# A two-layer hybrid encoder in hi/lo fp32r products: the feed-forward projections as 2x2 block products with seven multiplications

## The chip, the cores and the metric

The kernel runs on one core of one Trainium2 chip. The metric is the device time of one execution in microseconds (us), the median of several. PE is the matrix engine (PEld its weight loads), ACT the scalar engine, DVE the vector engine, POOL the general-purpose engine, SP the queue that issues DMAs. Each takes its instructions in order and waits at semaphores.

## The reference

The input x has 512 tokens of 1024 features. Layer 1 mixes by a gated delta rule over eight heads and by attention into 256 memory tokens; layer 2 by sliding-window attention over shared keys and values and by the same kind of memory attention. Each layer ends with a SwiGLU feed-forward network, and that is what is changed:

```python
def swiglu(h, w_gate_up, w_down):
    gate, up = jnp.split(h @ w_gate_up, 2, axis=-1)
    return (jax.nn.silu(gate) * up) @ w_down
```

Here h = rms_norm(x) is 512 x 1024, w_gate_up is 1024 x 5632, w_down is 2816 x 1024, and the result is added to x. Everything is float32.

## The kernel before

Activations lie transposed, features on the 128 partitions and the 512 tokens along the free axis, so that 1024 features are 8 tiles of 128 x 512 and the 2816 hidden features are 22. A float32 product is made of three fp32r products: every operand is split into hi (the value rounded to fp32r) and lo (what is left), and hi x hi, hi x lo and lo x hi are summed in one PSUM bank (`product`, L536 to L551). One matmul has a 128 x 128 weight tile as its stationary operand and 512 tokens streaming.

Weights come as blocks of up to 128 x 1024 into a ring of four slots `w_raw`. For each block SP loads (`load`), ACT writes `w_hi` (`upper`, L1044), POOL writes `w_lo = w_raw - w_hi` (`lower`, L480), and PE multiplies. ACT may write a slot only when PE is through with the block that was in it, and SP may load it when ACT and POOL are. All blocks of the program pass through this ring in one order, `_order`: the memory projections, the heads, out0, up00, down00, up01, down01, kv, swq, mq1, out1, up10, down10, up11, down11.

The feed-forward network of a layer is done in two halves of 11 hidden tiles (`HALF`). Of each hidden tile PE makes the gate tile and the up tile, 24 matmuls each, in banks 0 and 1. DVE multiplies both out of PSUM by the row factor `R_T` (L1426), ACT applies SiLU, DVE multiplies gate by up, ACT writes the hi part into `act_hi` and DVE the lo part (L1429). Then the down projection makes 8 output tiles from those 11, and DVE adds each to the residual `xT` (L1673). `residual` also squares each finished tile on ACT, sums the squares on DVE (L1686), and writes the hi and lo parts of the next layer's input; `row_sums` adds the squares over partitions on PE, and `rstd` makes R_T from it. The norm's gain is applied to the operand, R_T to the product. ffn, residual and out_tiles run as hardware loops with unrolled ends (`turns`); the last down projection also transposes each finished tile on PE (L894), and ACT copies it for the store.

Of the kernel before, what the change touches and what calls it, by code (L numbers as in the profile page):

```python
# [23 lines left out]
P = 128  # L24
# [25 lines left out]
          ("out0", 2 * KT), ("up00", 2 * HALF), ("down00", 2 * KT), ("up01", 2 * HALF), ("down01", 2 * KT),  # L50
          ("kv", 2), ("swq", SW_HEADS // QPB), ("mq1", MEM_HEADS), ("out1", 2 * KT),
          ("up10", 2 * HALF), ("down10", 2 * KT), ("up11", 2 * HALF), ("down11", 2 * KT)]
# [3 lines left out]
for _name, _count in _order:  # L56
    BLOCK0[_name], TILE0[_name] = _b, _n
    _b += _count
    _n += _count // 2 if _name.startswith(("out", "down")) else _count
N_BLOCKS, N_TILES = _b, _n  # L60
LAST = _order[-1][0]
OUT_SUB = (CAT // 2, CAT // 2)
DOWN_SUB = ((HALF + 1) // 2, HALF // 2)
RING = 4


def subtiles(block):

    for name, count in _order:
        if BLOCK0[name] <= block < BLOCK0[name] + count:  # L70
            half = (block - BLOCK0[name]) % 2
            return OUT_SUB[half] if name.startswith("out") else DOWN_SUB[half] if name.startswith("down") else KT
# [5 lines left out]
_c = 0  # L78
# [9 lines left out]
(IDENT, ONES, ONES64, TRIU, NEG_LOWER, LEVEL0) = range(6)  # L88
N_SQ = 6 + LEVELS - 1
# [34 lines left out]
def yoco_kernel(nc, x, mem, w_stream, w_out, w_down, w_ba, cols_in, squares_in, dist_in, out):  # L124
    with ExitStack() as ctx:
        def sb(name, shape, dt=F32):
            return ctx.enter_context(nc.sbuf_tensor(name, shape, dt))
# [4 lines left out]
        xT = sb("xT", [P, KT, SEQ])  # L132
        act_hi = sb("act_hi", [P, KT + CAT, SEQ], F32R)
        act_lo = sb("act_lo", [P, KT + CAT, SEQ], F32R)
        w_raw = sb("w_raw", [P, RING, KT * P])
        w_hi = sb("w_hi", [P, RING, KT * P], F32R)
        w_lo = sb("w_lo", [P, RING, KT * P], F32R)
        ws = sb("ws", [P, WS, SEQ])
        kmem = sb("kmem", [P, 2 * MEM_HEADS, MEM_LEN])
        vmem = sb("vmem", [P, 2 * MEM_HEADS, MT_ * P])  # L140
        sq_c = sb("sq_c", [P, N_SQ, P])
        cols = sb("cols", [P, N_COLS])
        dn_s = sb("dn_s", [P, 8, DN_HEADS * NT])
        state = sb("state", [P, P])
        st = sb("st", [P, 64])
# [3 lines left out]
        class S:  # L149
# [15 lines left out]
            m_sq = sem("m_sq")  # L165
            m_ln = sem("m_ln")
            m_rstd = sem("m_rstd")
            m_scaled = sem("m_scaled")
# [1704 lines left out]
```

## Time and profile before

| | us |
|---|---|
| median of 3 runs (1636.85 to 1640.55) | 1639.7 |
| the profiled execution | 1640.73 |
| its span, first to last instruction | 1638.9 |
| mean granted PE clock in it | 0.986 |

The profile gives each engine's busy time. Matmuls are pipelined, and the duration given for one (0.39 us for 512 columns) reaches over its successor's start; the distance between starts is what one costs in a row of them. Line numbers are often those of helpers: L1044 is every ACT operation, L1426 a DVE multiply, L1429 a subtraction, L1432 an operation of three inputs (scalar_tensor_tensor), L1435 a copy. So an operation is known by its tiles: `bank` is PSUM, `ws`, `xT`, `act_hi`, `act_lo`, `w_raw`, `w_hi` and `w_lo` are SBUF.

### The profile page before, as it was taken

How to read it: one execution, taken by the hardware profiler on the slowest of the kernel's cores; microseconds unless marked ns; L12 is line 12 of the kernel's file. 1: busy time of each engine (PE TensorE's matmuls, PEld its weight loads, DVE VectorE, ACT ScalarE, POOL GpSimd, SP SyncE). 2: the span in 40 equal slices, each digit the busy share in tenths (PEclk: the TensorE clock that was granted, in tenths of full speed). 3: DMA queues.
4: the chain of work that ended last, by engine and by line, in shares of the span. 5: the costliest groups of instructions: out<-in, count | busy, mean ns of one | idle time of the engine just before them, and what ended most of it. 6: DMA issues, size and time to landing. Idle time of an engine off the chain costs nothing.

```text
span 1638.9 us, 21277 instructions
## 1 busy us (share of the span) xinstructions
PE 1558.5 (95%) x7900; PEld 1277.1 (78%) x7900; DVE 624.2 (38%) x1014; ACT 586.6 (36%) x956; POOL 577.8 (35%) x286
## 2 busy tenths in 40 slices
PE   6899999999998989999999999887889999999998
PEld 6868878888787668888888887666668888888887
DVE  3336555665555432222122224677532222012210
ACT  6642243223332433322222234454533322222321
POOL 5531332223220234544434444211124443544442
PEclk9999999999999999999999999999999999999999
DMA  7411110111010123332333233111113332333222
GB/s 252 127 56 39 52 33 32 51 38 51 26 33 0 39 77 96 104 102 82 112 102 101 74 89 122 42 39 30 30 49 108 95 101 79 114 103 102 80 79 86
DMA packets 39208, 124.24 MB, mean 76 GB/s; under 512 B 4192, under 2 KB 5472, under 8 KB 39136
## 3 DMA queue, kind: packets, MB, share of 16 engines
q1 hardware_dynamic: 38976, 123.00, 25.0%
q8 instruction: 47, 0.77, 0.2%
q10 hardware_dynamic: 160, 0.26, 0.1%
q14 instruction: 25, 0.20, 0.0%
HBM read 120.89 MB, written 2.10 MB: 75 GB/s over the span
## 4 chain that ended last, share of the span: by engine, by line
PE 85%; DVE 6%; ACT 5%; issue 3%; DMA 0%; POOL 0%; SPq 0%; DVEq 0%; ACTq 0%
PE bank L548 66%; ACT ws L1044 4%; PE bank L713 3%; PE bank L711 2%; PE bank L699 2%; DVE ws L1426 1%; PE bank L977 1%; DVE ws L1432 1%; DVE act_lo L1432 1%; PE bank L847 1%; PE bank L810 1%; DVE ws L1435 1%; DVE ws L1429 1%; PE bank L736 1%; PE bank L1002 1%
## 5 line engine op out<-in xcount | busy, mean ns | idle before, releaser
L480 POOL TENSOR_TENSOR w_lo<-w_raw,w_hi 128x1024 fp32r<-128x1024 f32 (+1 forms) x250 | 537.8, 2168 | 949.8 <-ACT w_hi L1044 949.5
L548 PE MATMUL bank<-act_hi,w_hi 128*128 128x512 f32 (+1 forms) x1776 | 704.3, 397 | 10.0 <-POOL w_lo L480 4.4
L548 PE MATMUL bank<-act_hi,w_lo 128*128 128x512 f32 (+1 forms) x1776 | 681.0, 383 | 0.0
L548 PE MATMUL bank<-act_lo,w_hi 128*128 128x512 f32 (+1 forms) x1776 | 680.6, 383 | 0.0
L548 PEld LDWEIGHTS bank<-act_hi,w_hi 128*128 128x128 f32 x1776 | 336.2, 189 | 76.9 <-issue 7.8
L548 PEld LDWEIGHTS bank<-act_hi,w_lo 128*128 128x128 f32 x1776 | 335.6, 189 | 65.7
L548 PEld LDWEIGHTS bank<-act_lo,w_hi 128*128 128x128 f32 x1776 | 336.4, 189 | 63.8 <-issue 5.0
L1044 ACT ACTIVATE w_hi<-w_raw 128x1024 fp32r<-128x1024 f32 (+1 forms) x250 | 230.4, 953 | 89.1 <-PE bank L548 86.6
L1426 DVE TENSOR_TENSOR ws<-bank,ws 128x512 f32<-128x512 f32 x126 | 86.9, 690 | 371.5 <-PE bank L548 320.9
L1044 ACT ACTIVATE ws<-ws 128x512 f32<-128x512 f32 (+3 forms) x143 | 94.3, 670 | 189.2 <-DVE ws L1426 122.0
L1673 DVE TENSOR_TENSOR xT<-xT,bank 128x512 f32<-128x512 f32 (+1 forms) x48 | 33.0, 688 | 271.6 <-PE bank L548 271.6
L1044 ACT ACTIVATE act_hi<-ws 128x512 fp32r<-128x512 f32 (+1 forms) x52 | 32.8, 631 | 238.4 <-DVE ws L1426 238.1
L1044 ACT ACTIVATE ws<-bank 128x512 f32<-128x512 f32 x56 | 33.2, 593 | 164.1 <-PE bank L748 47.7
L1429 DVE TENSOR_TENSOR ws<-ws,bank 128x512 f32<-128x512 f32 (+1 forms) x96 | 61.8, 644 | 55.9 <-PE bank L713 55.7
L1435 DVE COPY ws<-bank 128x128 f32<-128x128 f32 (+4 forms) x94 | 44.7, 483 | 88.1 <-PE bank L548 54.1
L713 PE MATMUL bank<-ws 128*128 128x128 f32 x384 | 71.7, 278 | 2.0 <-DVE ws L1426 2.0
L699 PE MATMUL bank<-ws 128*128 128x128 f32 x384 | 58.5, 288 | 4.1 <-DVE ws L1429 3.5
L711 PE MATMUL bank<-ws 128*128 128x128 f32 x320 | 62.3, 276 | 0.0
L1145 ACT ACTIVATE ws<-bank,cols 128x512 f32<-128x512 f32 x24 | 16.5, 687 | 124.8 <-PE bank L548 124.8
L699 PEld LDWEIGHTS bank<-ws 128*128 128x128 f32 x384 | 50.8, 193 | 11.8 <-DVE ws L1429 7.1
L713 PEld LDWEIGHTS bank<-ws 128*128 128x128 f32 x384 | 56.9, 193 | 3.6 <-DVE ws L1426 3.6
L1044 ACT ACTIVATE ws<-xT 128x512 f32<-128x512 f32 (+1 forms) x24 | 15.2, 632 | 119.8 <-DVE xT L1673 119.8
(145 smaller groups left out, 1211.8 us busy)
## 6 DMA issues: line engine op xcount, KB each, us to landing
w_raw<-w_stream SPq DMA_DIRECT2D x154, 512.0 KB, 3.5
w_raw<-w_out SPq DMA_DIRECT2D x32, 384.0 KB, 3.2
w_raw<-w_down SPq DMA_DIRECT2D x32, 384.0 KB, 3.1
w_raw<-w_down SPq DMA_DIRECT2D x32, 320.0 KB, 3.2
ws<-x_in SPq DMA_DIRECT2D x1, 2048.0 KB, 8.4
ws<-mem_in SPq DMA_DIRECT2D x2, 512.0 KB, 4.0
out<-ws SPq DMA_DIRECT2D x1, 1024.0 KB, 4.2
sq_c<-squares_in SPq DMA_DIRECT2D x1, 768.0 KB, 6.3
```

What stands on the lines that cost most here:

```text
L480: nc.gpsimd.tensor_tensor(w_lo[:, s, 0:width * P], w_raw[:, s, 0:width * P], w_hi[:, s, 0:width * P].bitcast(F32), ALU.subtract).then_inc( ...
L548: mm = nc.tensor.matmul(acc, wt[:, c % RING, wsl], at[:, act0(k0 + k), off:off + n], start=(start and k == 0 and m == 0), stop=(stop and k ...
L699: mm = nc.tensor.matmul(bank[:, D[3 - g], i * P:(i + 1) * P], tt(MM, t), tt(TT, t), start=True, stop=True)
L711: nc.tensor.matmul(bank[:, D[4 + g], i * P:(i + 1) * P], tt(ZZ, t), tt(PM, t), start=True, stop=True)
L713: mm = nc.tensor.matmul(bank[:, D[4 + g], (2 + i) * P:(3 + i) * P], tt(PM, t), tt(ZZ, t), start=True, stop=True)
L1044: return nc.scalar.activation(out_, in_, func, **kw)
L1145: nc.scalar.activation(w(CQ + j), psum(j % 2), ACT.Copy, scale=conv_w(h, j, 3)).then_inc(S.cv_tap, 1)
L1426: return V.tensor_tensor(out_, x_, y_, ALU.mult)
L1429: return V.tensor_tensor(out_, x_, y_, ALU.subtract)
L1432: return V.scalar_tensor_tensor(out=out_, in0=x_, scalar=scalar, in1=y_, op0=op0, op1=op1)
L1435: return V.tensor_copy(out_, x_)
L1673: V.tensor_tensor(xT[:, k, :], xT[:, k, :], psum(j), ALU.add).then_inc(S.acc_free, 1)
```

## The change

Both projections of the feed-forward network are cut into units. An up unit makes one gate tile and one up tile, from the two halves of the 8 input tiles and for the two halves of the 512 tokens: a 2x2 by 2x2 block product, done with seven products instead of eight. A down unit makes output tiles m and m + 4 from one chunk of hidden tiles (6, 8 and 8 of the 22), in the same way. Per layer there are 22 up units and 12 down units (4 of them with 3 tiles a half, 8 with 4). A product is kn x 3 matmuls of 256 columns (kn is 4, or 3 in the chunk of 6).

The weight side needs four sums of 128 x (kn x 128), T1 to T4, that DVE makes from the raw weights, T1 and T2 into `wT`, T3 and T4 in place. ACT raises and POOL lowers seven blocks instead of four. The activation side needs four sums S1 to S4 of 256 columns for each pair of tiles; DVE makes them into `ST`, ACT writes their hi part for all four at once, POOL their lo part (for the last pair of a set DVE does it, one by one). The parts A11, A12 and A22 that enter unsummed get their lo part from DVE. Products accumulate in two PSUM banks per unit, X and Y, and are read out between products: ACT copies the first, third and fourth out, DVE adds the others.

The raw weights of a unit come with one DMA of 1 MB (768 KB in the chunk of 6) into half of `w_raw`, two units in flight. The loops of residual and ffn are unrolled on all engines. The SBUF map is written out by hand, with the feed-forward tiles G (gate), U (hidden, three tiles), ST and wT over tiles that are free at that time; the constant squares are reordered. Several semaphores are merged in pairs (`o_ln` and `o_rstd` into `o_rt`, and the like) with the same waits. The outputs are stored tile by tile. The kv product takes its tiles in the order in which they are finished (`DONE`), and its first weight blocks are raised by ACT after the last down unit's tile 7 is copied.

The core of the diff (new functions; the old ffn, residual and out_tiles go):

```diff
+CHUNKS = (6, 8, 8)
+PRODUCTS = (("A11", 0, 0, 0), ("A12", 0, 1, 1), ("S2", 1, 0, 0), ("S1", 1, 1, 1), ("S3", 2, 0, 0), ("S4", 2, 1, 1),
+            ("A22", 3, 0, 0))
+BLOCK_END = (2, 4, 6, 7)
...
+            # POOL
+            def unit_lower(unit, i):
+                pool.wait_ge(S.fh_done, 4 * unit.v + i + 1)
+                nc.gpsimd.tensor_tensor(ring_pair(w_lo, unit, i), raw_pair(unit, i),
+                                        ring_pair(w_hi, unit, i).bitcast(F32), ALU.subtract).then_inc(S.fl_done, 1)
+            def ffn(layer):
+                for i in range(3):
+                    unit_lower(Unit(layer, 0), i)
+                for n in range(N_UNITS):
+                    unit = Unit(layer, n)
+                    unit_lower(unit, 3)
+                    following = Unit(layer, n + 1) if n + 1 < N_UNITS else None
+                    if following:
+                        unit_lower(following, 0)
+                        unit_lower(following, 1)
+                    done = unit.prev
+                    if done and done.up and done.side and not pair_of(done).last:
+                        s_lower(pair_of(done))
+                    if following:
+                        unit_lower(following, 2)
...
+            # PE
+            def accumulator_free(unit, q):
+                if q == 0 and unit.n >= 2:
+                    older = unit.prev.prev
+                    if older.up:
+                        pe.wait_ge(S.u_dve, 4 * older.f + 4)
+                    else:
+                        pe.wait_ge(S.d_add, 7 * older.d + 7)
+                if q < 2:
+                    return
+                if not unit.up:
+                    pe.wait_ge(S.d_add, 7 * unit.d + q - 1)
+                elif q in (3, 6):
+                    pe.wait_ge(S.u_dve, 4 * unit.f + q // 3)
+                else:
+                    pe.wait_ge(S.u_act, 3 * unit.f + {2: 1, 4: 2, 5: 3}[q])
+            def unit_products(unit, q):
+                name, i, half, side = PRODUCTS[q]
+                acc = bank[:, 4 + 2 * (unit.v % 2) + side, 0:HT]
+                pe.wait_ge(S.fl_done, 4 * unit.v + i + 1)
+                accumulator_free(unit, q)
+                for k in range(unit.kn):
...
+                    for m, (wt, a_) in enumerate(((w_hi, a_hi), (w_hi, a_lo), (w_lo, a_hi))):
+                        mm = nc.tensor.matmul(acc, wt[:, slot(unit, i), wsl], a_,
+                                              start=(q in (0, 1, 3) and k == 0 and m == 0),
+                                              stop=(k == unit.kn - 1 and m == 2), skip_group_check=True)
+                mm.then_inc(S.prod, 1)
...
+            # ACT, an up unit
+                        if after_up:
+                            silu(prev, 1)
+                        copy_out(unit, 0)
+                        if after_up and prev.side:
+                            hidden_upper(prev, "A22")
...
+                        unit_upper(unit, 3)
+                        unit_upper(nxt, 0)
+                        copy_out(unit, 2)
+                        if n:
+                            silu(unit, 0)
+                        copy_out(unit, 3)
+                        unit_upper(nxt, 1)
+                        if after_up and prev.side:
+                            upper_s(pair_of(prev))
+                        unit_upper(nxt, 2)
...
+                        hidden_upper(unit, "A12" if unit.side else "A11")
...
+            # DVE
+            def unit_sums(unit, names):
+                raw, n = raw_of(unit), unit.kn * P
+                b11, b21, b12, b22 = (raw[:, i, 0:n] for i in range(4))
+                for name in names:
+                    if name == "T1":
+                        dve.wait_ge(unit_loaded[unit.v % 2], 16 * (unit.v // 2 + 1))
+                        if due(unit.v):
+                            dve.wait_ge(S.fl_done, 4 * unit.v - 2)
+                        sub(wT[:, 1, 0:n], b12, b11).then_inc(S.t_op, 1)
+                    elif name == "T2":
+                        dve.wait_ge(S.t_op, 4 * unit.v + 1)
+                        sub(wT[:, 0, 0:n], b22, wT[:, 1, 0:n]).then_inc(S.t_op, 1)
+                    elif name == "T3":
+                        sub(b12, b22, b12).then_inc(S.t_op, 1)
+                    else:
+                        dve.wait_ge(S.t_op, 4 * unit.v + 2)
+                        dve.wait_ge(S.fl_done, 4 * unit.v + 1)
+                        sub(b21, b21, wT[:, 0, 0:n]).then_inc(S.t_op, 1)
+            def gate_sum(unit):
+                g1 = halves(unit)[0]
+                dve.wait_ge(S.prod, 7 * unit.v + 2)
+                dve.wait_ge(S.u_act, 3 * unit.f + 1)
+                V.tensor_tensor(g1, g1, banks_of(unit)[1], ALU.add).then_inc(S.u_dve, 1)
+            def gate_scale(unit):
+                g1 = halves(unit)[0]
+                dve.wait_ge(S.u_dve, 4 * unit.f + 1)
+                mul(g1, g1, w(R_T)[:, 0:HT]).then_inc(S.f_sc, 1)
+            def gate_last(unit):
+                dve.wait_ge(S.prod, 7 * unit.v + 7)
+                mul(halves(unit)[1], banks_of(unit)[0], w(R_T)[:, HT:]).then_inc(S.u_dve, 1)
+            def hidden(unit, half):
+                g_, u_ = halves(unit)[half], halves(unit)[2 + half]
+                dve.wait_ge(S.f_sc, 3 * unit.f + 3 - half)
+                dve.wait_ge(S.f_silu, 2 * unit.f + 1 + half)
+                mul(u_, u_, g_).then_inc(S.f_hid, 1)
...
+            # DVE, an up unit behind an up unit
+                        gate_last(prev)
+                        unit_sums(unit, ("T4",))
+                        hidden(prev, 1)
+                            if prev.side:
+                                a_lower(pair, "A12", hB[:, 0:HT])
+                                s_op(pair, "S2", hA, hB)
+                                s_op(pair, "S1", hA, hB)
+                            else:
+                                s_op(pair, "S3", hA, hB)
+                                a_lower(pair, "A11", hA[:, 0:HT])
+                            gate_sum(unit)
+                            gate_scale(unit)
+                        if after_up and prev.side:
+                            s_op(pair, "S4", hA, hB)
+                            a_lower(pair, "A22", hB[:, HT:])
+                        unit_sums(nxt, ("T1", "T2"))
+                        up_sum(unit, 1)
+                            up_scale(unit, 1)
+                        unit_sums(nxt, ("T3",))
+                        up_sum(unit, 0)
+                        up_scale(unit, 0)
+                        hidden(unit, 0)
```

The lines with `#` name the engine and are not in the file. In a down unit the DVE does, beside the T sums, seven `down_add`s, each `xT` half plus a bank; the first down unit of a chunk also finishes the last pair of hidden tiles (`hidden`, S2, S1, S4, `a_lower`, and `last_lower` for S2, S1 and S4).

## Rows read from the trace of the kernel before

**Rows 1.** The page's first part: busy us (share) x instructions of each engine.

```profile
PE 1558.5 (95%) x7900; PEld 1277.1 (78%) x7900; DVE 624.2 (38%) x1014; ACT 586.6 (36%) x956; POOL 577.8 (35%) x286
```

**Rows 2.** The page's chain of waits, share of the span by line.

```profile
PE bank L548 66%; ACT ws L1044 4%; PE bank L713 3%; PE bank L711 2%; PE bank L699 2%; DVE ws L1426 1%; PE bank L977 1%; DVE ws L1432 1%; DVE act_lo L1432 1%; PE bank L847 1%; PE bank L810 1%; DVE ws L1435 1%; DVE ws L1429 1%; PE bank L736 1%; PE bank L1002 1%
```

**Rows 3.** Windows, first feed-forward stretch: us, busy us (x), clock, DMA, GB/s.

```profile
646.00:1004.50 358.50, 358.50 (x1581) 296.56 (x1581) 82.94 (x119) 109.33 (x142) 158.10 (x76) 1.00 0.33 97
```

**Rows 4.** Timeline of PE, 512 columns: start us, us, engine, line, tiles.

```profile
620.21 0.39 PE L548 MATMUL bank<-act_hi,w_hi 128*128 128x512 f32 x1
...
635.85 0.39 PE L548 MATMUL bank<-act_hi,w_hi 128*128 128x512 f32 x1
```

**Rows 5.** Timeline of PE, products of 256 columns.

```profile
20.12 0.28 PE L548 MATMUL bank<-act_hi,w_hi 128*128 128x256 f32 x1
...
22.99 0.28 PE L548 MATMUL bank<-act_hi,w_hi 128*128 128x256 f32 x1
```

**Rows 6.** Groups of POOL by shape, 600 to 1000 us: busy us, mean ns.

```profile
L480 POOL TENSOR_TENSOR w_lo<-w_raw,w_hi 128x1024 fp32r<-128x1024 f32 x44 | 104.7, 2399 | 130.1 <-ACT w_hi L1044 130.1
L480 POOL TENSOR_TENSOR w_lo<-w_raw,w_hi 128x768 fp32r<-128x768 f32 x26 | 47.7, 1842 | 90.3 <-ACT w_hi L1044 90.3
```

**Rows 7.** Groups of POOL by shape, whole span.

```profile
L507 POOL TENSOR_TENSOR act_lo<-ws,act_hi 128x512 fp32r<-128x512 f32 x3 | 3.9, 1294 | 54.6 <-ACT act_hi L1044 54.6
```

**Rows 8.** Groups of ACT by shape, whole span.

```profile
L1044 ACT ACTIVATE w_hi<-w_raw 128x1024 fp32r<-128x1024 f32 x154 | 157.0, 1047 | 24.5 <-PE bank L548 22.1 <-issue 2.1 <-DMA w_raw<-w_stream 0.2
L1044 ACT ACTIVATE ws<-ws 128x256 f32<-128x256 f32 x16 | 6.7, 416 | 9.1 <-DVE ws L1435 8.8
L1044 ACT ACTIVATE ws<-bank,cols 128x256 f32<-128x256 f32 x8 | 3.8, 475 | 12.1 <-PE bank L578 12.1
```

**Rows 9.** Groups of DVE by shape, whole span.

```profile
L1426 DVE TENSOR_TENSOR ws<-bank,sq_c 128x256 f32<-128x256 f32 x96 | 37.8, 418 | 11.8 <-PE bank L699 11.6
L1686 DVE TENSOR_TENSOR ws<-ws 128x512 f32<-128x512 f32 x21 | 14.5, 693 | 17.0 <-ACT ws L1044 17.0
```

**Rows 10.** Timeline of POOL in three stretches.

```profile
585.67 6.07 POOL L480 TENSOR_TENSOR w_lo<-w_raw,w_hi 128x768 fp32r<-128x768 f32 x3
...
655.92 2.40 POOL L480 TENSOR_TENSOR w_lo<-w_raw,w_hi 128x1024 fp32r<-128x1024 f32 x1
...
1044.19 2.59 POOL L480 TENSOR_TENSOR w_lo<-w_raw,w_hi 128x1024 fp32r<-128x1024 f32 x1 [9.63 <-ACT w_hi L1044]
```

**Rows 11.** Timeline of DVE in the same stretches.

```profile
586.25 1.54 DVE L1435 COPY ws<-ws 128x512 f32<-128x512 f32 x1 [0.70 <-ACT ws L1044]
587.72 2.32 DVE L1432 SCALAR_TENSOR_TENSOR act_lo<-xT,cols,act_hi 128x512 fp32r<-128x512 f32 x1
...
656.67 0.69 DVE L1426 TENSOR_TENSOR ws<-bank,ws 128x512 f32<-128x512 f32 x1 [3.34 <-PE bank L548]
657.47 1.40 DVE L1426 TENSOR_TENSOR ws<-ws 128x512 f32<-128x512 f32 x1
...
1044.48 0.55 DVE L1435 COPY ws<-bank 128x384 f32<-128x384 f32 x1
1044.95 2.37 DVE L1432 SCALAR_TENSOR_TENSOR ws<-ws,cols 128x512 f32<-128x512 f32 x1
```

**Rows 12.** Waits of PE: us in total, times, longest us.

```profile
PE bank L548 <- DVE act_lo L1429: 2.8, 2, 1.4
```

**Rows 13.** Windows view of two other stretches, columns as in rows 3.

```profile
16.00:19.40 3.40, 3.40 (x16) 3.40 (x17) 0.00 (x0) 2.61 (x6) 3.12 (x2) 0.52 0.69 206
...
1100.00:1200.00 100.00, 85.20 (x464) 63.74 (x463) 60.52 (x92) 50.66 (x140) 15.04 (x6) 0.93 0.09 25
```

## What the change does to the time, predicted

> **What bounds the kernel now.** I read the page's engine line first: PE is busy for 1558.5 of 1638.9 us, DVE, ACT and POOL each for 35 to 38% [rows 1]. Then the chain of waits by line: 66% of the span is L548, the hi/lo products [rows 2]. The windows show the first feed-forward stretch: PE busy 358.5 of 358.5 us at full clock, DMA at a third [rows 3]. So there PE sets the time and nothing else does; POOL has 158 of 358 us of work, DVE 83, ACT 109. Its products stand 0.2266 us apart: (635.85 - 620.21) / 69 starts [rows 4]. Per layer there are 22 x 2 x 8 x 3 up and 8 x 22 x 3 down matmuls, 1584; both layers 3168 x 0.2266 = 717.9 us. That is the part of the span that the change replaces.
>
> **What PE gains.** Seven block products in place of eight, but 256 columns wide. An up unit is 7 x 4 x 3 = 84 matmuls; per layer 22 such, 8 down units of 84 and 4 of 63, in all 2772, both layers 5544. The trace has this shape in the memory projection: from 20.12 to 22.99 us lie 24 starts, 0.1196 us each [rows 5]. Two of them cost 0.239 against 0.2266 for one of 512 columns, so the eighth saved shrinks: 5544 x 0.1196 = 663.1 us, 54.8 less. An up unit takes PE 10.05 us, a six-tile down unit 7.53. If nothing else moved, this would be the result. (The Trainium skill, "TensorE: Matmul & The Clock Gate", section Back-to-back issue gap, gives N/2.4 + 2.5 ns for a lone warm matmul: 0.109 and 0.216 us. By it the saving would be 684 - 605 = 79 us. The rows are 0.010 us longer in both widths, and the measurement decides.)
>
> **What the helpers must do per unit.** POOL lowers three weight blocks of 1024 columns and one of 512, and on every second up unit 1024 columns of S operands. A lowering of 1024 columns takes 2.40 us and of 768 1.84 [rows 6], of 512 1.29 [rows 7]. Up unit: 3 x 2.40 + 1.29 = 8.49, plus 1.20 on average, 9.69 of PE's 10.05. Before, it was 4.80 per 10.9 us. ACT: three uppers of 1.05, one of 0.63, three copies out of PSUM, two SiLUs, 1.5 operand copies at about 0.42 to 0.47, half a 1.05: about 7.2 us [rows 8]. It fits. DVE: four weight sums of 512 columns at 0.69, and 12.5 operations of 256 at 0.42 (gate_sum, up_sum x2, gate_last; three scalings, two hidden, two S sums, 1.5 a_lower): 8.0 us [rows 9]. By itself it fits too. DMA moves the same weights, and has two thirds free [rows 3].
>
> **What does not fit: POOL and DVE beside each other.** At 655.92 POOL starts a 2.40 us lowering. Inside it a DVE multiply out of PSUM runs in its usual 0.69. The next multiply has both inputs in SBUF; it starts at 657.47 and takes 1.40, ending at 658.87, which is 0.55 after POOL's end at 658.32 [rows 10, 11]. At 1044.95 the same: 2.37 us for an operation of 0.75, ending 0.54 behind POOL; the copy from PSUM just before took its 0.55. At 586.25 and 587.72, with POOL's queue full, two DVE operations take 1.54 and 2.32: three POOL lowerings stand in 6.07 us, 0.55 more than 3 x 1.84. So one waits for the whole of the other, and with both queues full they take turns, one for one. I found 49 DVE operations on SBUF alone that touched a POOL one, and none that did its work inside it. (The Trainium skill, "SBUF — State Buffer", section SBUF: two separate sides, says this of DVE operations with two SBUF inputs against GpSimd: an exclusive lock, held for the whole instruction. The trace agrees for two SBUF tensors, with 0.55 us behind POOL's end, and shows that a PSUM input escapes. It is the rule that speaks against this change.)
>
> Before, an up pair had two such DVE operations in 10.9 us. Now an up unit has four of 512 columns (T1 to T4) and 8.5 of 256. Each holds 0.55, or 0.55 - (0.69 - 0.42) = 0.28 us for 256 columns [rows 9, 11]: 4 x 0.55 + 8.5 x 0.28 = 4.58. With POOL: **9.69 + 4.58 = 14.27 us per up unit, against 10.05 on PE.** That is the floor. On top comes the time in which neither holds: gate_last and one up_sum read PSUM (0.42 each) and stand between SBUF operations in DVE's queue, and they wait for PE. The others fall inside POOL's work. I laid two units out in the order of the queues; POOL's are u3 (this unit's last block), n0, n1, n2 (the next one's), with s ahead of n2 on even units. Times from the end of one n2: T4 0.55, hidden 0.9, S3 1.25, a_lower 1.6 (all while POOL waits for ACT's u3, which waits for T4), u3 2.9, gate_scale 3.2, n0 5.5, T1 and T2 6.7 (POOL's n1 waits for T2), up_sum 7.0, up_scale 7.35, T3 8.0, n1 10.3, up_scale 10.6, n2 12.9. The even unit, with s (2.40) and three small operations more, came to 17.6, as T4 there also waits. The mean is 15.2, and I take it. Behind the DVE operation that waits for n2 stands gate_last; silu, hidden_upper and copy_out wait for it on ACT, and for copy_out PE's third product: PE stands still there for 2 to 4 us a unit. The other end is that every PSUM operation (1.7 us) and two ACT turns (0.8 each) lie bare: 17.5.
>
> Down units: seven adds read PSUM and escape; only the T sums collide. Eight tiles: 8.49 + 4 x 0.55 = 10.7, by hand 11.0 (PE 10.05); six tiles: 3 x 1.84 + 1.01 (384 columns, 2.17 ns each below 1.29) + 4 x 0.42 = 8.2, taken 8.4. The first of each chunk also has hidden, three S sums, three last_lower and two a_lower: 9 x 0.28 more, less one T sum, 12.7 and 10.3. Each also is a chain: S2 waits for hidden, last_lower for ACT, PE for both, and at each link a POOL lowering can come in between. I take 15 and 12 (PE waits about 5 us at each chunk's change).
>
> **Sum.** 44 x 15.2 = 669; 4 x 15 + 12 x 11 = 192; 2 x 12 + 6 x 8.4 = 74. In all 935 us for 717.9: +217.
>
> **Edges.** Out to up: the last residual tile now goes through halves, S2, S1, S4 and their lowerings before products 2 to 6; PE waits there today 2.8 us at two places [rows 12]. I take 2.5 more each; nothing to 6 is possible. The sums (h copies, S, squares) in the out projection have room, since POOL needs 3.7 of a tile's 12 x 3 x 0.2266 = 8.16 us. Into kv: its first weight block is raised only behind the copies of tile 7 and then costs 2.40 on POOL, some 3 us that are hidden now. End: two tiles are turned behind the last product, where one was; about 0.5. Merged semaphores, the SBUF map and unrolled loops: nothing (the memory projection is unrolled, at the distances of rows 5). Together +8.
>
> The profiled execution took 1640.7 (span 1638.9, so 1.8 around it), 1.0 above the median of 1639.7. 1640.7 + 217 + 8 = 1866, against the median **1865 us**, 13.7% slower. With the floors (14.3, 10.7, 8.2, 12.7, 10.3): 629 + 51 + 128 + 21 + 49 = 878, so 1800. With 17.5, 12.5, 9.5, 18, 14: 770 + 72 + 150 + 28 + 57 = 1077, with edges of 12 about 2010.
>
> **Rivals.**
> *PE still sets the time (faster).* The SBUF operations of DVE would find gaps of POOL, or the turn-taking costs only the small overlap. Then 1640 - 55 + 8 + 6 chunk changes x 2 = 1605. For it: POOL alone fits (9.69 in 10.05), and before, only two of 44 hidden multiplies were held back by POOL. Against it: gaps of 0.36 us in 10.05 do not take 4.58.
> *Only half of it shows.* If the unit is PE's 10.05 plus half of the excess, 12.1 for up units and PE's own for down: 1640 - 55 + 44 x 2.1 + 20 = 1700. For it: the six small operations behind gate_sum could pass while POOL waits for ACT.
> *The clock falls as well (slower still).* With PE busy 10.05 of 15.2 us, the granted clock may go to 1.2 GHz between. The memory projection's start shows it: clock 0.52 from 16 to 19.4 us [rows 13]. At that level a unit's products take twice as long, 20 us. If it holds for a third of them, PE needs 13.4 plus the waits of 4 us or so that it can't make up: about 17.5 per up unit, 1965 in all. Against: with PE busy 85% the stretch 1100 to 1200 us still had 0.93 [rows 13].
>
> **How the numbers follow.** The exclusion at full or nearly full clock 0.77 (own range 1800 to 1960), clock 0.08, half 0.06, PE-bound 0.09. To hold eight in ten, the range goes from 1775 to 1970: it leaves out the PE-bound case, half, and the far end. Faster by over 0.2% (what a measurement of this kernel tells from no change): 0.09; within 0.2%: 0.01; slower: 0.90.
>
> **What would show it.** After: PE's share in the feed-forward stretches near 65%, products still 0.12 apart within a run; DVE's T sums (128x512, both inputs in SBUF) with a mean well over 0.69, 1.5 us or more, with single ones of 2.9; 256-column multiplies of SBUF likewise; gate_sum and the down adds from PSUM at 0.42. POOL lowerings of 1024 columns near 2.6 to 2.9. POOL's busy plus DVE's own work near the whole stretch. Starts of like products of two neighbouring up units 15 us apart, of down units 11. PE's waits name DVE ops, ACT's copies and w_lo. Wrong would be: T sums of 0.69 beside a running POOL; PE busy over 90%; up units at 10 to 11 us.

## The result, and the profile after

The changed kernel takes **1877.0 us** (median of 4 runs, 1872.7 to 1878.3) against 1640.1 for the kernel before, measured beside it (4 runs): 14.4% slower, ratio 1.144 [1.142, 1.147]. Forecast were 1865 us and 13.7%.

The page of the changed kernel, its engine line and its chain by line, which answer to [rows 1, 2]:

```profile
PE 1611.9 (86%) x10276; PEld 1424.3 (76%) x10276; DVE 1342.8 (72%) x1870; ACT 779.0 (42%) x1350; POOL 915.9 (49%) x428
...
PE bank L718 20%; PE bank L1099 15%; DVE U L1758 7%; DVE wT L1761 4%; ACT ws L1238 4%; DVE w_raw L1761 4%; DVE ST L1761 3%; PE bank L883 2%; PE bank L881 2%; PE bank L869 2%; DVE ws L1764 1%; DVE U L2135 1%; DVE ws L1758 1%; PE bank L1017 1%; DVE G L1758 1%
```

PE has fewer columns to compute and is busy for longer; DVE's busy time has more than doubled. The products of L548 held 66% of the chain. Now the block products of the feed-forward (L1099) hold 15% and all other hi/lo products (L718) 20%; most of the rest stands at DVE's lines, 28% of the chain in all. The windows view of the two feed-forward stretches of the changed kernel (columns as in [rows 3]):

```profile
646.00:1125.00 479.00, 385.94 (x2776) 371.97 (x2775) 436.49 (x528) 198.24 (x325) 320.57 (x144) 0.91 0.21 73
1360.00:1860.00 500.00, 412.17 (x2878) 392.65 (x2877) 436.36 (x534) 205.09 (x335) 335.60 (x152) 0.91 0.22 74
```

In [rows 3] PE was busy for all of it at clock 1.00, with DVE at 83 of 358.5 us. Here DVE is the full one, with 436 of 479 us, and the granted clock is 0.91. Why it is full stands in its groups. DVE, then POOL, of the changed kernel by shape (busy us, mean ns):

```profile
L1758 DVE TENSOR_TENSOR U<-U,ws 128x256 f32<-128x256 f32 x88 | 109.4, 1245 | 2.7
L1761 DVE TENSOR_TENSOR w_raw<-w_raw,wT 128x512 f32<-128x512 f32 x60 | 105.8, 1764 | 0.0
L1761 DVE TENSOR_TENSOR wT<-w_raw 128x512 f32<-128x512 f32 x60 | 98.6, 1643 | 0.0
L2170 DVE TENSOR_TENSOR xT<-xT,bank 128x256 f32<-128x256 f32 x168 | 67.5, 414 | 55.5 <-PE bank L1099 54.1
L2120 DVE TENSOR_TENSOR G<-G,bank 128x256 f32<-128x256 f32 x44 | 18.3, 415 | 7.8 <-PE bank L1099 5.5 <-ACT G L1238 2.3
```

```profile
L665 POOL TENSOR_TENSOR w_lo<-w_raw,w_hi 128x1024 fp32r<-128x1024 f32 x120 | 310.8, 2590 | 49.6 <-ACT w_hi L1238 49.5
L665 POOL TENSOR_TENSOR w_lo<-wT,w_hi 128x1024 fp32r<-128x1024 f32 x60 | 151.0, 2516 | 132.5 <-ACT w_hi L1238 132.5
```

Operations of one width have different prices. With a `bank` (PSUM) among the inputs, 256 columns take 0.413 to 0.416 us in every group. With both inputs in SBUF the mean is 1.245 in the group above, and 512 columns take 1.64 (T1) and 1.76 (T4) where [rows 9] have 0.693. Some groups on SBUF alone keep their price (`op_b_lo_dn<-U,op_b_hi_dn`, 0.421), so the form only makes an operation liable; whether it pays depends on what POOL does at that moment. The difference between a group's mean and the price alone (0.42 us for 256 columns, 0.55 for 384, 0.69 for 512), times its count, added over all groups of the feed-forward, is 400 us. I call it DVE's **held time** below. The timeline shows single operations. DVE and POOL of the changed kernel around 707 us:

```profile
707.86 2.85 DVE L1761 TENSOR_TENSOR wT<-w_raw 128x512 f32<-128x512 f32 x1
710.74 0.69 DVE L1761 TENSOR_TENSOR wT<-w_raw,wT 128x512 f32<-128x512 f32 x1
712.02 0.42 DVE L2135 TENSOR_TENSOR U<-U,bank 128x256 f32<-128x256 f32 x1 [0.59 <-PE bank L1099]
712.48 0.42 DVE L1758 TENSOR_TENSOR U<-U,ws 128x256 f32<-128x256 f32 x1
712.82 2.88 DVE L1761 TENSOR_TENSOR w_raw<-w_raw 128x512 f32<-128x512 f32 x1
715.63 0.41 DVE L2139 TENSOR_TENSOR U<-U,bank 128x256 f32<-128x256 f32 x1
```

```profile
706.13 4.03 POOL L665 TENSOR_TENSOR w_lo<-w_raw,w_hi 128x512 fp32r<-128x512 f32 x2 [1.29 <-ACT w_hi L1238]
712.61 2.55 POOL L665 TENSOR_TENSOR w_lo<-wT,w_hi 128x1024 fp32r<-128x1024 f32 x1 [2.45 <-ACT w_hi L1238]
```

T1, the sum that starts at 707.86, ends at 710.71, 0.55 us behind POOL's end (706.13 + 4.03 = 710.16). T3, from 712.82, ends at 715.70, 0.54 behind 715.16. T2, from 710.74, finds POOL silent and takes its 0.69. The chain of waits of the changed kernel shows the price on the path:

```profile
706.99 5.01 PE bank L1099 x24
712.00 0.02 issue
712.02 0.43 DVE U L2135
712.45 0.02 issue
712.48 0.42 DVE U L1758
712.90 2.80 DVE w_raw L1761
715.70 0.34 DVE U L2139
```

T3, held for 2.2 us, stands ahead of the up_sum that PE's next products need. The chain's first piece shows something more: 24 matmuls in 5.01 us are 0.21 us each, not 0.12. The granted clock of this stretch (706.99 to 712.00) is 0.57: PE has come out of its wait at the lower of its two levels, 1.2 GHz, for most of it.

### The profile page after: what moved, and what is told of

Read it like the earlier page. It is cut to its first block, busy times and chain, and to the rows that moved or that the text cites. A ratio compares the mean times of both kernels' runs of the same rounds, so it can differ in the third digit from the quotient of the medians.

```text
span 1875.8 us, 27072 instructions
## 1 busy us (share of the span) xinstructions
PE 1611.9 (86%) x10276; PEld 1424.3 (76%) x10276; DVE 1342.8 (72%) x1870; ACT 779.0 (42%) x1350; POOL 915.9 (49%) x428
## 4 chain that ended last, share of the span: by engine, by line
PE 52%; DVE 28%; issue 13%; ACT 5%; POOL 0%; DMA 0%; DVEq 0%; ACTq 0%; SPq 0%
PE bank L718 20%; PE bank L1099 15%; DVE U L1758 7%; DVE wT L1761 4%; ACT ws L1238 4%; DVE w_raw L1761 4%; DVE ST L1761 3%; PE bank L883 2%; PE bank L881 2%; PE bank L869 2%; DVE ws L1764 1%; DVE U L2135 1%; DVE ws L1758 1%; PE bank L1017 1%; DVE G L1758 1%
## 5 line engine op out<-in xcount | busy, mean ns | idle before, releaser
L665 POOL TENSOR_TENSOR w_lo<-w_raw,w_hi 128x1024 fp32r<-128x1024 f32 (+3 forms) x204 | 437.0, 2157 | 165.2 <-ACT w_hi L1238 165.2
L608 POOL TENSOR_TENSOR w_lo<-w_raw,w_hi 128x1024 fp32r<-128x1024 f32 (+1 forms) x98 | 221.3, 2272 | 541.4 <-ACT w_hi L1238 541.4
L1099 PE MATMUL bank<-op_s_hi,w_hi 128*128 128x256 f32 x1056 | 338.5, 321 | 142.7 <-ACT G L1238 79.5
L1099 PEld LDWEIGHTS bank<-op_s_hi,w_hi 128*128 128x128 f32 x1056 | 231.4, 219 | 161.3 <-issue 143.4
L1238 ACT ACTIVATE w_hi<-w_raw 128x1024 fp32r<-128x1024 f32 (+3 forms) x302 | 270.7, 917 | 150.9 <-DVE w_raw L1761 126.1
L1099 PE MATMUL bank<-op_s_hi,w_lo 128*128 128x256 f32 x1056 | 328.2, 311 | 0.0
L1099 PE MATMUL bank<-op_s_lo,w_hi 128*128 128x256 f32 x1056 | 328.1, 311 | 0.0
L718 PE MATMUL bank<-act_hi,w_hi 128*128 128x512 f32 (+1 forms) x704 | 288.3, 409 | 9.9 <-POOL w_lo L608 4.4
L718 PE MATMUL bank<-act_lo,w_hi 128*128 128x512 f32 (+1 forms) x704 | 267.0, 379 | 0.0
L718 PE MATMUL bank<-act_hi,w_lo 128*128 128x512 f32 (+1 forms) x704 | 266.5, 379 | 0.0
L1099 PEld LDWEIGHTS bank<-op_s_lo,w_hi 128*128 128x128 f32 x1056 | 232.6, 220 | 0.5 <-issue 0.5
L1099 PEld LDWEIGHTS bank<-op_s_hi,w_lo 128*128 128x128 f32 x1056 | 231.3, 219 | 0.0
L718 PEld LDWEIGHTS bank<-act_hi,w_hi 128*128 128x128 f32 x704 | 135.4, 192 | 36.5 <-issue 6.9
L718 PEld LDWEIGHTS bank<-act_hi,w_lo 128*128 128x128 f32 x704 | 134.9, 192 | 26.7
L718 PEld LDWEIGHTS bank<-act_lo,w_hi 128*128 128x128 f32 x704 | 135.5, 193 | 23.3 <-issue 4.1
L1099 PE MATMUL bank<-op_b_hi_up,w_hi 128*128 128x256 f32 x352 | 100.8, 286 | 14.3 <-DVE U L2135 14.3
L1758 DVE TENSOR_TENSOR U<-U,ws 128x256 f32<-128x256 f32 x88 | 109.4, 1245 | 2.7
```

Of the source, the lines that this page charges most:

```text
L608: nc.gpsimd.tensor_tensor(w_lo[:, s, 0:width * P], w_raw[:, s, 0:width * P], w_hi[:, s, 0:width * P].bitcast(F32), ALU.subtract).then_inc( ...
L665: nc.gpsimd.tensor_tensor(ring_pair(w_lo, unit, i), raw_pair(unit, i), ring_pair(w_hi, unit, i).bitcast(F32), ALU.subtract).then_inc(S.fl_ ...
L718: mm = nc.tensor.matmul(acc, wt[:, c % RING, wsl], at[:, act0(k0 + k), off:off + n], start=(start and k == 0 and m == 0), stop=(stop and k ...
L1099: mm = nc.tensor.matmul(acc, wt[:, slot(unit, i), wsl], a_, start=(q in (0, 1, 3) and k == 0 and m == 0), stop=(k == unit.kn - 1 and m == ...
L1238: return nc.scalar.activation(out_, in_, func, **kw)
L1758: return V.tensor_tensor(out_, x_, y_, ALU.mult)
```

## The experiments

The times are of one run each, but for the two that say otherwise. The changed kernel's own four runs lie within 5.6 us, so single runs that differ from it by less than that show no difference. The kernel before took 1636.5 beside the first four, 1639.5 beside the fifth, 1641.8 beside the next three and 1639.9 beside the last two. "Up unit" is the mean of 38 distances between two gate_last operations (G<-bank,ws), 15.15 us in the changed kernel. Where a run puts a tile into a bank that the transposes of the last down projection used, these go through two or three banks instead of four.

### No DVE operation with two SBUF inputs

```diff
-                        sub(b12, b22, b12)
+                        sub(b12, b22, bank[:, 3, 0:n])   # shortened; so in every sum, scaling, hidden product and lowering
```

The values of the feed-forward layers are left out (the second input is a constant).

> The changed kernel with one edit: every DVE sum, scaling, hidden product and lowering of the feed-forward that had two SBUF inputs takes its second input from a PSUM bank that holds a constant 0.03 (so the values of the feed-forward are left out). Counts, shapes, waits and POOL's work stay. Theory (DVE on two SBUF inputs and POOL exclude each other): DVE operations of 512 columns fall from 1.1 to 1.8 us to 0.69, those of 256 to 0.42, POOL's 1024 columns from 2.59 to 2.40, up units come from 15.15 to 10.1 to 10.8 us, the kernel to 1605 to 1650. Rival (it is the amount of work: POOL 9.69 and DVE 8.0 us of a 10.05 us unit, and the chain over ACT): durations may fall but the unit stays at 13 us or more, the kernel above 1740.

**1624.4 us.** Up units 10.05. DVE's operations have the same widths, and there are two more of them (the constant is written once per layer). Windows view, then a group each of DVE and POOL:

```profile
700.00:1000.00 300.00, 292.54 (x2417) 291.47 (x2416) 210.13 (x453) 167.52 (x269) 257.05 (x126) 0.99 0.29 102
```

```profile
L1761 DVE TENSOR_TENSOR wT<-w_raw,bank 128x512 f32<-128x512 f32 x120 | 81.9, 683 | 1.9
```

```profile
L665 POOL TENSOR_TENSOR w_lo<-w_raw,w_hi 128x1024 fp32r<-128x1024 f32 x120 | 289.3, 2411 | 30.7 <-ACT w_hi L1238 29.9
```

POOL at 257 and DVE at 210 of 300 us run side by side, each at its own price. So neither the amount of work nor DVE's sequence makes the 237 us; where an input lies does.

### POOL's weight lowerings shortened

```diff
-    nc.gpsimd.tensor_tensor(ring_pair(w_lo, unit, i), raw_pair(unit, i), ...)
+    nc.gpsimd.tensor_tensor(ring_pair(w_lo, unit, i)[:, :, 0:8], raw_pair(unit, i)[:, :, 0:8], ...)
```

Left out: all but 8 columns of each part of w_lo in the feed-forward layers.

> The changed kernel with POOL's lowerings of the feed-forward weight blocks cut to 8 columns a piece (the rest of their lo parts is left out); DVE's operands stay in SBUF, POOL keeps 2.4 us of S lowering per two up units. Theory (exclusion): DVE has SBUF nearly to itself, its 512-column sums are at 0.69 to 0.8; up units at 10.1 to 10.8 us, kernel 1600 to 1640. Rival (DVE's own 8 us and its chain with ACT and PE set the unit): 1700 or more.

**1617.8 us**, up units 10.21, held time 30 us. The same cure from the other side: DVE's code is the changed kernel's, and with POOL at 59 of 300 us it runs free. It also shows about how much the scheme could win in this program: even with the weight lowering almost free it is 1.1% under before.

### R_T alone in PSUM

```diff
-                mul(g1, g1, w(R_T)[:, 0:HT])
+                mul(g1, g1, bank[:, 3, 0:HT])     # and both scalings of u
```

> The changed kernel with the row factors R_T also in a free PSUM bank, and gate_scale and the two up_scales reading them there: 3 of 8.5 small SBUF operations per up unit escape, nothing else moves. Theory (exclusion): the floor falls by 3 x 0.28 = 0.84 us per up unit, 37 us in all, and more where the scaling waited for a whole POOL lowering (its mean is 1.25 instead of 0.42, 0.83 x 88 + 0.65 x 44 = 102 us of waiting in all): 1775 to 1840. Rival (durations only show waiting that something else sets): 1870 to 1880.

**1872.4 us: a miss.** DVE's groups by shape, two freed and two not:

```profile
L1760 DVE TENSOR_TENSOR U<-U,bank 128x256 f32<-128x256 f32 x88 | 36.8, 420 | 2.7
L1763 DVE TENSOR_TENSOR op_b_lo_dn<-U,op_b_hi_dn 128x256 fp32r<-128x256 f32 x44 | 53.6, 1218 | 4.2 <-ACT op_b_hi_dn L1238 2.9
L1763 DVE TENSOR_TENSOR op_a_lo_dn<-U,op_a_hi_dn 128x256 fp32r<-128x256 f32 x22 | 30.5, 1388 | 0.0
L1763 DVE TENSOR_TENSOR w_raw<-w_raw,wT 128x512 f32<-128x512 f32 x60 | 126.4, 2107 | 0.0
```

The freed scalings escape: 109.4 us became 36.8. But op_b_lo_dn, 0.421 before in the changed kernel, now takes 1.218, op_a_lo_dn 1.388 after 0.418, T4 2.107 after 1.764. The POOL instruction catches the next SBUF operation in the queue. Held time goes from 400 to 360 us, up units to 15.32, and the kernel is as slow as the changed one. The largest of PE's waits, in the changed kernel and then here:

```profile
PE bank L1099 <- ACT G L1238: 79.5, 36, 3.2
```

```profile
PE bank L1099 <- DVE G L2122: 123.9, 36, 6.8
```

L2122 is gate_sum. It stands in DVE's queue behind the hidden product and the operand lowerings that are now caught.

### Filling PE's wait

```diff
+                if q == 2 and unit.up and unit.n:
+                    for k in range(12):
+                        nc.tensor.matmul(bank[:, 3, 0:HT], ...)   # shortened; 256 columns into a bank that nothing reads
                 accumulator_free(unit, q)
```

> The changed kernel with twelve more matmuls of 256 columns (1.43 us at full clock) on PE ahead of the wait of each up unit's third product, into an unused bank. Tests whether the lower clock (0.91 in the feed-forward, 753 of 5544 starts 0.21 us apart, 71 us in all) lies on the path. If it does: the clock rises to 0.97 or more and the time falls by 20 to 60 us, to 1820 to 1860, although PE has 62 us more work. If it does not: 1875 to 1940.

**1869.5 us.** Windows view, to be held against 0.91 and 244.58 us (x1785) for PE in the changed kernel:

```profile
700.00:1000.00 300.00, 253.47 (x1982) 244.47 (x1981) 277.78 (x337) 121.27 (x200) 212.06 (x97) 0.98 0.22 77
```

The clock comes back from 0.91 to 0.98, for at most 7.5 us of the 237. As a ratio to the kernel before beside it (1636.5) the gain is 0.2%, hardly more than single runs differ by. It lies between the two expectations, and near no effect: the low clock is mostly spent where PE would have stood anyway.

### T1, T2 and R_T in PSUM

```diff
-                        sub(wT[:, 1, 0:n], b12, b11).then_inc(S.t_op, 1)
+                        sub(bank[:, 3, 0:n], b12, b11).then_inc(S.t_op, 1)
-                        sub(wT[:, 0, 0:n], b22, wT[:, 1, 0:n]).then_inc(S.t_op, 1)
+                        sub(bank[:, 2, 0:n], b22, bank[:, 3, 0:n]).then_inc(S.t_op, 1)
```

DVE also makes w_lo of T1 and T2 (from PSUM), which POOL gives up; R_T stands in bank 0.

> The changed kernel with T1 and T2 written to two PSUM banks instead of SBUF, their lo part made by DVE (one PSUM input, 1024 columns, about 1.2 us) and no longer by POOL, and R_T read from PSUM as in the run before. Same values as the full computation. Per up unit POOL has 7.29 us in place of 9.69, and the SBUF-only operations of DVE are T1, T3, two hidden, two S sums and 1.5 lowerings: 2 x 0.55 + 5.5 x 0.28 = 2.64. Theory (exclusion): floor 9.93 us, about PE's own 10.05, so up units at 10.5 to 11.5 and the kernel at 1630 to 1700. Rival (amount of work): DVE has 1.2 us more, 9.2 us per unit; the time stays above 1750.

**1775.0 us** (median of 4 runs, ratio to before 1.082 [1.080, 1.084]): 102 us won, but the theory's size is missed by 75, and the time lies above 1750, where the rival (amount of work) had put it. This time alone doesn't decide between them; the run in which DVE does POOL's work does, further down. Held time 179 us. Most up units take 12.6 us and some 17 to 18, mean 13.69. Part of what was freed again went to others:

```profile
L1763 DVE TENSOR_TENSOR U<-U,G 128x256 f32<-128x256 f32 x88 | 108.2, 1230 | 2.9 <-ACT G L1241 1.4
L1766 DVE TENSOR_TENSOR op_b_lo_dn<-U,op_b_hi_dn 128x256 fp32r<-128x256 f32 x44 | 54.8, 1246 | 3.4 <-ACT op_b_hi_dn L1241 2.0
```

### POOL's instructions in halves

```diff
-    nc.gpsimd.tensor_tensor(ring_pair(w_lo, unit, i), ...)
+    for b in range(2):                       # and s_lower likewise
+        nc.gpsimd.tensor_tensor(ring_pair(w_lo, unit, i)[:, b:b + 1, :], ...)
```

> The changed kernel with every subtraction of 1024 columns on POOL in the feed-forward layers (three of four weight blocks, and the pair lowerings of four blocks) issued as two of 512 columns; the work and its order are otherwise the same. Theory A (capacity: POOL's subtractions and DVE's operations with two SBUF inputs exclude each other, and the sum of both is what fills an up unit): POOL's own time rises from 9.69 to eight of 1.29 us = 10.3 an up unit, so the unit gets no shorter, 15.0 to 15.8 us, and the kernel 1870 to 1905. Rival B (latency: what costs is that one DVE operation stands behind one whole POOL instruction of 2.5 us, 8.5 times a unit): the waits are halved, an up unit comes down to 12 to 13.5 us and the kernel to 1750 to 1810.

**1861.7 us.** Up units 15.18, held time 367 us: the up units don't shorten, as capacity has it. The kernel is 15 us faster, 8 more than the range allowed. About 10 of them are in the down units: the four of a chunk take 34.6 and 43.5 us instead of 37.2 and 45.7. In exchange POOL is held more: 512 columns take a mean of 1.490 us, against 1.29 in [rows 7]. POOL's group of 512 columns:

```profile
L668 POOL TENSOR_TENSOR w_lo<-w_raw,w_hi 128x512 fp32r<-128x512 f32 x300 | 438.9, 1490 | 79.6 <-ACT w_hi L1245 79.5
```

### POOL's work given to DVE

```diff
-                nc.gpsimd.tensor_tensor(ring_pair(w_lo, unit, i), raw_pair(unit, i), ...)
+                sub(ring_pair(w_lo, unit, i), raw_pair(unit, i), ...)   # DVE, at the same places; s_lower too
```

> The changed kernel with every one of POOL's feed-forward subtractions (weight blocks and pair lowerings) issued by DVE instead, in the same order; POOL has nothing to do in the feed-forward layers beyond the three pair lowerings beside the out tiles. Theory A (exclusion): DVE's own work in an up unit is 8.0 us as its instructions run alone, and it gets 7 x 512 columns of weights and half of 4 x 256 columns at 0.67 to 0.69 us per 512 = 5.4 us more, 13.4 in all, with nothing to wait for on POOL: up units 13.0 to 13.8 us instead of 15.15, down units of kn 4 at 10.4 and of kn 3 at 8.7; the kernel 1780 to 1820, so faster than the changed one although its busiest helper has been given two thirds more work. DVE's 512-column subtractions should then read 0.69 and its 256-column ones 0.42. Rival B (the two engines run beside each other and what costs is DVE's own count of instructions): DVE busy for 1343 us already, and 44 x 5.4 us more of it puts the kernel at 2050 or above.

**1727.7 us**: 149 us faster than the changed kernel, with the engine that was full doing two engines' work. Its page and window, then three of DVE's groups:

```profile
PE 1560.3 (90%) x10276; PEld 1373.0 (80%) x10276; DVE 1211.8 (70%) x2158; ACT 775.8 (45%) x1350; POOL 275.6 (16%) x140
...
700.00:1000.00 300.00, 269.36 (x2091) 260.87 (x2090) 276.56 (x505) 141.65 (x236) 0.00 (x0) 0.97 0.26 89
```

```profile
L1748 DVE TENSOR_TENSOR w_lo<-w_raw,w_hi 128x1024 fp32r<-128x1024 f32 x120 | 146.3, 1219 | 0.0
L1748 DVE TENSOR_TENSOR wT<-w_raw 128x512 f32<-128x512 f32 x60 | 41.0, 684 | 0.0
L1745 DVE TENSOR_TENSOR U<-U,ws 128x256 f32<-128x256 f32 x88 | 37.0, 422 | 1.4
```

288 instructions more, 131 us less busy: of DVE's 873 us in the two stretches after the change, 400 were held time. Here it is 1 us. It went 52 us under the range's lower end of 1780, for a reason in the timeline of this kernel (DVE):

```profile
703.68 0.42 DVE L1745 TENSOR_TENSOR U<-U,ws 128x256 f32<-128x256 f32 x1
704.01 1.22 DVE L1748 TENSOR_TENSOR w_lo<-w_raw,w_hi 128x1024 fp32r<-128x1024 f32 x1
705.15 0.42 DVE L1745 TENSOR_TENSOR U<-U,G 128x256 f32<-128x256 f32 x1
705.49 0.42 DVE L1745 TENSOR_TENSOR G<-bank,ws 128x256 f32<-128x256 f32 x1
```

In these rows an operation of 0.42 us is followed after 0.33 to 0.34, one of 1.22 after 1.14. My sum took every duration in full, and 1.37 for 1024 columns: 13.4 for an up unit that took 11.93.

### More in PSUM, and halves

```diff
-                a(G[:, f % 2, part], G[:, f % 2, part], ACT.Silu).then_inc(S.f_silu, 1)
+                a(bank[:, 1, part], G[:, f % 2, part], ACT.Silu).then_inc(S.f_silu, 1)
-                mul(u_, u_, g_).then_inc(S.f_hid, 1)
+                mul(u_, u_, bank[:, 1, HT * half:HT * (half + 1)]).then_inc(S.f_hid, 1)
```

> The version with the sums T1 and T2 and R_T in PSUM (1775 us) and two things more: silu's output goes to PSUM bank 1, so that hidden = U x G has a PSUM input, and POOL's 1024-column subtractions are split in halves. SBUF-only DVE operations left in an up unit: T1, T3 and 3.5 of 256 columns = 2.8 us; POOL 1.5 x 2.58 + 1.29 + 1.29 = 6.5 us; together 9.3 us, under PE's 10.1. If capacity alone counts, up units come to 10.5 and the kernel to 1640; if each collision still costs its turn (as the 1775 us showed), up units come to 12 to 13 and the kernel to 1700 to 1750. No gain at all against 1775 would say that PE's wait sits elsewhere (ACT's order).

**1692.7 us**, up units 11.74, held time 103 us; PE at 275 of 300 us and clock 0.98. It is the fastest of the new scheme's versions that compute every value, a little under the 1700 to 1750 that "each collision still costs its turn" expected, and still 3.1% slower than before. The two edits weren't run apart.

### The gate's sum ahead of the operand sums

```diff
                             hidden(prev, 1)
+                            gate_sum(unit)
+                            gate_scale(unit)
                             dve.wait_ge(S.f_hid, 2 * prev.f + 2)
```

On the version of 1692.7 us, and then on the changed kernel alone.

> The version of 1692.7 us (T1, T2, R_T and silu's output in PSUM, POOL in halves) with gate_sum and gate_scale of an up unit issued right behind the previous unit's last hidden product, ahead of the operand lowerings and the sums S, for which nothing waits before the down units. There PE stood 31 us in 16 waits for gate_sum, up to 2.9 us each. Theory (what is left is the place in DVE's order where the collisions fall): those waits go, up units come from 11.7 to 10.5 to 11.2 and the kernel to 1650 to 1680, still not under before's 1640, because the first unit, the hand-overs between chunks and the sums of the down units stay. Rival (DVE and POOL together are full): the wait moves to the next thing that PE needs, u2's sum or the row of weights, and the time stays within 8 us of 1693.

> The changed kernel with that same reordering alone. Theory (capacity: POOL's 9.7 us and DVE's SBUF-only 4.6 us exclude each other, 14.3 an up unit, and the units take 15.15): at most 0.9 us a unit can be won by any order, so up units of 14.3 to 15.2 and 1840 to 1880. Rival (the order of DVE's program, not the exclusion's sum, makes the price): up units of 12 to 13.5 and 1760 to 1810.

**1700.7 us** (median of 4 runs, ratio to before 1.038 [1.035, 1.041]) and **1876.1 us** (up units 15.09). The first is a miss and the rival's case (7.7 us from 1693). PE's waits of the two versions, the one of 1692.7 us and then this:

```profile
PE bank L1109 <- DVE G L2138: 31.4, 16, 2.9
PE bank L1109 <- DVE U L2153: 10.0, 16, 0.6
```

```profile
PE bank L1109 <- DVE U L2153: 30.7, 20, 1.8
```

The wait for the gate's sum is gone and stands, in the same size, at the sum of u. On the changed kernel too the order is worth nothing.

### The runs together

```
version                         us      up unit  either  held time  SBUF-only DVE operations
changed                         1877.0  15.15    14.22   400        732
R_T in PSUM                     1872.4  15.32    13.37   360        600
PE's wait filled                1869.5  14.89    14.22   405        732
order only                      1876.1  15.09    14.13   403        732
POOL in halves                  1861.7  15.18    14.16   367        732
T1, T2, R_T in PSUM             1775.0  13.69    9.80    179        464
POOL's work on DVE              1727.7  11.93    10.32   1          1020
and silu in PSUM, halves        1692.7  11.74    9.33    103        376
and gate's sum first            1700.7  11.92    9.41    124        376
no DVE op with two SBUF inputs  1624.4  10.05    9.29    0          0
POOL short                      1617.8  10.21    7.32    30         732
```

Held time and operations are counted over DVE's tensor_tensor groups of the feed-forward layers by the rule given above. "Either" is worked out from the timelines of POOL and DVE: the us of an up unit in which POOL runs or DVE runs an operation on SBUF alone, over the same 38 distances. In the rows with POOL at work it is what the two need when they take turns. The time follows the held time, but for the version in which DVE itself is the full one.

The column says what the arithmetic of the prediction and of the expectations was worth. It forecast 14.27 for the changed kernel (measured 14.22), 14.27 - 3 x 0.28 = 13.43 with R_T in PSUM (13.37), 9.93 with T1, T2 and R_T (9.80) and 9.3 with silu too (9.33). What the expectations had wrong is the rest of the unit, in which neither runs: 0.93 us in the changed kernel, but 1.95, 3.89 and 2.41 in these three. So freeing operations does lower the floor by the full sum, and the up unit doesn't come down to it.

## Why the prediction was right

**The exclusion, its size.** Shown: with the inputs in PSUM, with POOL short, and with POOL idle, 253, 259 and 149 us go. The last is the one that computes all values and leaves no room for the amount of work: DVE has 288 operations more and the kernel is faster. The few places that the trace of before had of it [rows 10, 11] gave the same 0.55 us behind POOL's end. The rule of the Trainium skill ("SBUF — State Buffer", section SBUF: two separate sides) that was weighed there agrees: DVE's groups of 256 columns with a PSUM input stay at 0.41 to 0.42 us in every run, and only those on SBUF alone grow. The two rivals in which DVE finds gaps (1605, 1700) fall.

**The up unit.** 15.2 was forecast; 38 distances in the two layers have the mean 15.15. The split by hand, 12.9 and 17.6 in turn, did not come: a chunk of eight has 13.8, 14.6, 15.3, 14.6, 14.4, 16.4, 17.0. So the mean was right and the schedule behind it was not. That POOL's 9.69 and DVE's 4.58 add up, as the sum put it, is measured: one or the other runs for 14.22 us of the unit (14.27 forecast), and neither for 0.93 (15.2 - 14.27 = 0.93 by the hand layout). Halves and the order agree (15.18, 15.09: neither helps). But the second part was not a constant: with R_T in PSUM the sum falls to 13.37 as it should, and the unit stays at 15.32.

**The down units and the first ones.** From the last up unit of a chunk to the first of the next, less one up unit, are 37.2 us with three block rows per unit (forecast 12 + 3 x 8.4 = 37.2) and 45.7 with four (15 + 3 x 11 = 48). The last chunk's down units took 54.4 and 49.5. The first up unit of a layer was not set apart in the sum and took 21.3 us (from the first product at 652.06 to gate_last at 673.33), 6 us over a mean one. With POOL short it took 16.4 us, also 6 over, so that excess isn't the exclusion's. The middle chunks came out 2 us under the forecast each and the last ones 6.4 and 1.5 over; so part of what makes the total so close is that these errors cancel, which is luck. Together the stretches are 476.7 + 472.0 = 948.7 us for 717.9: +231, forecast +217.

**The edges.** The profiled span is 1875.8, so 927.1 lie outside those stretches, 921.0 before: +6, forecast +8.

**The clock.** It was a rival (1965 us), and it came in part: granted 0.91, 753 of the 5544 products 0.19 to 0.23 us from the next. The step "PE's share near 65%" failed by this: 244.6 of 300 us are 82%, of which 1785 x 0.1196 = 213.5 are what its work takes at full clock. The hand layout had PE at full speed and waiting for 2 to 4 us, which did not fit the prediction's own sum: 15.2 - 10.05 leaves 5.15. Measured per up unit are 3.7 us in which PE stands (starts more than 0.3 us apart) and 15 starts that come 0.09 us late, 1.4 us together; with 10.05 they make 15.15. So the wait was shared between standing and running slowly, and filling it bought 7.5 us at most. That the clock has no term of its own in the sum was right in size.

**PE's gain.** 54.8 us less PE work was right, but of it only 19 us (1617.8 against 1636.5) show even with POOL short: the up units take 10.21, not 10.05, and the first unit and chunk changes the rest. The PE-bound rival's 1605 was too low by its edges.

**The other signs.** T1 and T4 at 1.64 and 1.76 us with single ones of 2.88, gate_sum and the down adds at 0.415: as listed. T2 and T3, at 1.15 and 1.06, stayed below the 1.5 named, and POOL's 1024 columns, at 2.52 to 2.59, at or under the lower end.

**What stays open.** Why freeing some operations gives so little: 132 of 732 SBUF operations freed (R_T) took 40 us of held time and nothing clear of noise from the kernel's (4.6 us; the ratio to the kernel before stays at 1.144), 268 freed with 68 lowerings moved off POOL took 222 and 102. What is shown is that the time in which neither engine runs on SBUF grows, and that with R_T in PSUM PE's waits gather at gate_sum. My reading, which is argued and not shown, is that DVE's queue is in order and POOL waits for DVE's own sums by way of ACT, so a DVE operation that is done sooner makes the next one arrive while POOL runs. No run takes that loop apart, and gate_sum first was not tried together with R_T alone in PSUM.

## What to carry to other kernels

Before adding elementwise work to an engine that has room, look at what it shares with the other engines: here two of them that were busy for 35 to 38% of the span could not do 8.0 and 9.7 us of work in a unit of 10 us side by side, because DVE's operations with two SBUF inputs and POOL's subtractions on SBUF take turns. If they must be, put one input of DVE's into PSUM for all the operations that meet POOL (the run that did so left the values out, and 1692.7 us is how far this went with them), or give the whole work to one engine; freeing some of them, reordering them or cutting POOL's in halves gave little each. Add up what the two need in turns: that is a floor, and it came out within 0.15 us of the count in four versions. The unit can lie 1 to 4 us above it. A mean duration far over the same shape elsewhere in the profile is a wait that the busy share hides.

## What the runs showed of the hardware that was not expected

- One engine alone beat the two as the change had them (1727.7 against 1877.0 us): POOL's feed-forward work on DVE took 1.22 us per 1024 columns, where POOL takes 2.41 undisturbed.
- Back to back, DVE operations start 0.08 us before the one ahead has ended (0.42 us long and 0.34 apart, 1.22 long and 1.14 apart in the rows above); a sum of durations overstates a full queue.
- POOL is held too: 2.59 us a lowering after the change, 2.41 with nothing to collide with. Over the feed-forward POOL's work took 43 us longer than with DVE's inputs in PSUM, where DVE was held for 400. In halves POOL pays more, 1.49 us for 512 columns against 1.29.
- A copy from SBUF to SBUF is caught as well: 1.54 us at 586.25 in [rows 11], where the same copy takes 0.43 alone.
- A result in PSUM is no escape, only an input is: T1 with two inputs in SBUF and its output in PSUM still took 1.15 us (bank<-w_raw, mean of 60 in the version of 1692.7 us), T2 beside it, with a PSUM input, 0.695.
